# The second attention's projections: latent keys normed inside the query projection, tile by tile, with q's norm factor applied at the mask

## The reference

```python
kv_a = rms_norm(x, kv_norm) @ kv_w_a                      # 256 latent + 64 rotary columns
c_kv = rms_norm(kv_a[..., :256], kv_c_norm)
kv   = (c_kv @ kv_w_b)        # 8 heads x (128 key + 128 value)
k    = rms_norm(concat(kv keys, k_pe), kv_k_norm); rotary on its last 64 columns
q    = rms_norm((rms_norm(h @ w_q_a, q_a_norm) @ w_q_b), q_norm)   # 8 heads x 192, rotary on the last 64
p    = masked_softmax(q . k * 192 ** -0.5)
out  = (p @ v) @ w_out
```

## Time and profile before

| | us |
|---|---|
| median of three runs (lowest, highest) | 1888.21 (1884.53, 1888.35) |
| the profiled execution | 1888.43 |
| its span, first to last instruction | 1886.6 |
| TensorE busy in the span | 1729.1 (92%) |
| VectorE, ScalarE busy | 1229.9 (65%), 817.3 (43%) |
| mean granted clock of TensorE | 0.960 |

### The profile page before, as it was taken

The page is one execution under the profiler, slowest core; times in us unless marked ns, Lnnn a source line. Parts: engine busy times, 40 slices in busy tenths (PEclk is TensorE's granted clock), DMA queues, the critical chain, the costliest instruction groups (busy, mean ns, idle before and its releaser), DMA issues.

```text
span 1886.6 us, 29289 instructions
## 1 busy us (share of the span) xinstructions
PE 1729.1 (92%) x11365; PEld 1591.6 (84%) x11365; DVE 1229.9 (65%) x1751; ACT 817.3 (43%) x1199; POOL 39.3 (2%) x23
## 2 busy tenths in 40 slices
PE   7869999997697999999989869999899989689998
PEld 7857799996577999999988769999899989479997
DVE  4778566666767566666668956565766554866665
ACT  4556444335344333534353054334533344754433
POOL 0000000000005000000000000000000000000000
PEclk9979999998798999999999989999999999889999
DMA  7610345453223545455434034545354545035544
GB/s 265 212 45 1 99 171 198 174 193 102 99 68 133 192 175 200 146 190 198 177 142 161 1 122 168 195 172 200 146 189 178 196 138 178 2 101 202 199 171 162
DMA packets 53291, 285.93 MB, mean 152 GB/s; under 512 B 5872, under 2 KB 6128, under 8 KB 30704
## 3 DMA queue, kind: packets, MB, share of 16 engines
q1 hardware_dynamic: 52224, 281.46, 41.5%
q0 software_dynamic: 1008, 3.67, 0.5%
HBM read 284.05 MB, written 1.05 MB: 151 GB/s over the span
## 4 chain that ended last, share of the span: by engine, by line
PE 82%; DVE 11%; ACT 4%; issue 2%; DMA 0%; DVEq 0%; SPq 0%; ACTq 0%
PE bank L827 18%; PE bank L828 17%; PE bank L829 17%; PE bank L987 9%; PE bank L956 3%; PE bank L958 3%; PE bank L960 3%; DVE proj L1743 3%; PE bank L841 2%; PE bank L1044 1%; PE bank L1003 1%; ACT whi L437 1%; PE bank L1024 1%; DVE nmax L1477 1%; DVE att L1475 1%
## 5 line engine op out<-in xcount | busy, mean ns | idle before, releaser
L827 PE MATMUL bank<-hthi,whi 128*128 128x256 f32 x2144 | 607.9, 284 | 1.9 <-DVE wlo L1274 1.8
L828 PE MATMUL bank<-htlo,whi 128*128 128x256 f32 x2144 | 607.2, 283 | 0.0
L829 PE MATMUL bank<-hthi,wlo 128*128 128x256 f32 x2144 | 607.1, 283 | 0.0
L1268 DVE TENSOR_TENSOR wlo<-raw,whi 128x2048 fp32r<-128x2048 f32 x175 | 401.4, 2294 | 97.5 <-ACT whi L437 97.3
L827 PEld LDWEIGHTS bank<-hthi,whi 128*128 128x128 f32 x2144 | 411.7, 192 | 7.3 <-DVE wlo L1274 2.2
L828 PEld LDWEIGHTS bank<-htlo,whi 128*128 128x128 f32 x2144 | 411.6, 192 | 4.7
L829 PEld LDWEIGHTS bank<-hthi,wlo 128*128 128x128 f32 x2144 | 411.6, 192 | 0.0
L437 ACT ACTIVATE whi<-raw 128x2048 fp32r<-128x2048 f32 x175 | 333.9, 1908 | 34.8 <-PE bank L829 27.3
L509 ACT ACTIVATE tr<-tr 128x256 f32<-128x256 f32 x132 | 55.1, 418 | 657.8 <-DVE tr L1352 657.8
L1352 DVE TENSOR_TENSOR tr<-bank,rb 128x512 f32<-128x512 f32 x132 | 91.2, 691 | 231.8 <-PE bank L829 231.6
L1274 DVE TENSOR_TENSOR wlo<-raw,whi 128x1024 fp32r<-128x1024 f32 x174 | 214.5, 1233 | 25.5 <-ACT whi L445 25.1
(11 more groups left out here) (241 smaller groups left out, 2088.9 us busy)
## 6 DMA issues: line engine op xcount, KB each, us to landing
raw<-in_stream SPq DMA_DIRECT2D x176, 1024.0 KB, 5.3
raw<-in_stream SPq DMA_DIRECT2D x176, 512.0 KB, 3.5
wide<-in_wide POOLq DMA_DIRECT2D x7, 512.0 KB, 4.1
x<-in_x SPq DMA_DIRECT2D x1, 1024.0 KB, 5.4
out<-x SPq DMA_DIRECT2D x2, 512.0 KB, 2.9
wide<-in_const SPq DMA_DIRECT2D x1, 960.0 KB, 15.5
const<-in_const SPq DMA_DIRECT2D x1, 897.0 KB, 12.7
cols<-in_cols SPq DMA_DIRECT2D x1, 340.0 KB, 7.8
```

The lines of the kernel that those rows point to most:

```text
L827: nc.tensor.matmul(out, whi_, mhi, start=start, stop=False)
L828: nc.tensor.matmul(out, whi_, mlo, start=False, stop=False)
L829: return nc.tensor.matmul(out, wlo_, mhi, start=False, stop=stop)
L1268: V.tensor_tensor(wlo[:, s, 0:UA], raw[:, s, 0:UA], whi[:, s, 0:UA].bitcast(F32), ALU.subtract)\
```

## The change

- U_QA's piece b is split ahead of op_bq on ScalarE and VectorE; the eviction of U_KVA stands behind op_bq's first pair. The transposes of the latent keys (op_ckv) are issued by TensorE inside the step of U_QA, ahead of its chunk 6. Their high and low parts go to the buffers hidhi and hidlo (otherwise a feed-forward block's), not hthi and htlo, and come before the eviction of U_QA.
- The four KVB and QB units run as `step_by_tile`: all chunks of tile 0, then all of tile 1. The end of tile 0 raises a new semaphore s_half, upon which ScalarE evicts it (`evict_first`) while tile 1 runs. Tile 0 of the next unit waits for ScalarE's eviction only, tile 1 for VectorE's. U_KVB waits for both at its start. The transposes of op_qa come between U_KVB and U_KVB+1.
- k's sums and scaling come ahead of VectorE's eviction of U_QB+1. q's squares are taken by ScalarE per head and tile with an accumulator, 16 instructions of 192 columns in place of two of 1536, eight after U_QB and eight after the k copies; VectorE's sums go away.
- q isn't scaled by its norm factor. The factor times 192^-0.5 is the scalar of the mask instruction, which becomes one per tile. The rotary part of q is formed one tile at a time, and the low part of U_MO's piece a stands behind it, ahead of the q copies.

```diff
-            operand("op_bq", [(c, col("b_attn_norm", c)) for c in range(DC)], U_KVA + 1)
+            hi_b(U_KVA)
+            hi_a(U_QA)
+            norm(2)
+            hi_b(U_QA)
+            operand("op_bq", [(c, col("b_attn_norm", c)) for c in range(DC)], U_KVA + 1,
+                    after_first=lambda: evict(U_KVA, lambda t, u, c, w: kva[:, t, c:c + w], 2))
...
-            step(U_QA, lambda t, u, c, w: qa[:, t, c:c + w], 2)
+            hi_a(U_KVB)
+            hi_b(U_KVB)
+            operand("op_ckv", [(c, col("kv_c_norm", c)) for c in range(2)], 0, out=hidhi)
+            evict(U_QA, lambda t, u, c, w: qa[:, t, c:c + w], 2)
...
-            operand("op_ckv", [(c, col("kv_c_norm", c)) for c in range(2)], U_QA + 1)
+            hi_a(U_KVB + 1)
+
+            def evict_first(u, dst):
+
+                act.wait_ge(s_half, u - U_KVB + 1)
+                for j, (c, w) in enumerate(STEPS[u][2]):
+                    ins = nc.scalar.activation(dst(0, u, c, w), acc[plan[u][0][0][j]][:, 0:w], ACT.Copy)
+                ins.then_inc(s_eva, 1)
...
+            def q_squares(u):
+
+                act.wait_ge(s_eva, plan[u][2])
+                act.wait_ge(s_evd, plan[u][3])
+                for t in range(NT):
+                    for h in range(4 * (u - U_QB), 4 * (u - U_QB) + 4):
+                        at = 6144 + (4 * t + h % 4) * QK
+                        ins = nc.scalar.activation(tr[:, at:at + QK], q2[:, t, h, :], ACT.Square,
+                                                   accum_out=ss[:, 16 + 8 * t + h:17 + 8 * t + h])
+                return ins
+
+            evict_first(U_KVB, kv_out)
+            hi_b(U_KVB + 1)
             operand("op_qa", [(2 + c, col("q_a_norm", c)) for c in range(3)], U_QA + 1)
-            for u in (U_KVB, U_KVB + 1):
-                step(u, lambda t, u, c, w: kv[:, t, 4 * (u - U_KVB) + c // 256:4 * (u - U_KVB) + (c + w) // 256, :])
+            hi_a(U_QB)
+            evict_first(U_KVB + 1, kv_out)
+            hi_b(U_QB)
+            hi_a(U_QB + 1)
+            hi_b(U_QB + 1)
+            act.wait_ge(s_eva, plan[U_KVB + 1][2])
             act.wait_ge(s_evd, plan[U_KVB + 1][3])
-            act.wait_ge(s_eva, plan[U_KVB + 1][2])
             for t in range(NT):
                 ins = nc.scalar.activation(tr[:, 3072 + t * 1024:3072 + (t + 1) * 1024].rearrange("p (h n) -> p h n", h=H2),
                                            kv[:, t, :, 0:NOPE], ACT.Square)
             ins.then_inc(ev["k2_sq"], 1)
...
-            step(U_QB, q2_out)
+            evict_first(U_QB, q2_out)
+            own(q_squares(U_QB))
             act.wait_ge(ev["k2_ss"], 1)
             sqrt("k2n", 16, QK, EPS)
-            step(U_QB + 1, q2_out)
-            act.wait_ge(s_evd, plan[U_QB + 1][3])
-            act.wait_ge(s_eva, plan[U_QB + 1][2])
-            for t in range(NT):
-                nc.scalar.activation(tr[:, t * 1536:(t + 1) * 1536].rearrange("p (h n) -> p h n", h=H2),
-                                     q2[:, t, :, :], ACT.Square).then_inc(ev["q2_sq"], 1)
-            act.wait_ge(ev["q2_ss"], 1)
-            sqrt("q2n", 16, QK, EPS, 16)
+            hi_a(U_MO)
+            evict_first(U_QB + 1, q2_out)
...
+            own(q_squares(U_QB + 1))
+            sqrt("q2n", 16, QK, EPS, 16)
             attention("mla")
...
+            def step_by_tile(u, hi, lo, k0):
+
+                kk, pitch, pieces = STEPS[u]
+                s, end = u % 2, pieces[-1][0] + pieces[-1][1]
+                banks, before, _, _ = plan[u]
+                pe.wait_ge(s_loa, u + 1)
+                for t in range(NT):
+                    if t == 0 or u == U_KVB:
+                        pe.wait_ge(s_eva, plan[before][2])
+                    if t == 1 or u == U_KVB:
+                        pe.wait_ge(s_evd, plan[before][3])
+                    lhs = slice(t * P, (t + 1) * P)
+                    for k in range(kk):
+                        if t == 0 and k == kk - 1:
+                            pe.wait_ge(s_lob, u + 1)
+                        for j, (c, w) in enumerate(pieces):
+                            sl = slice(k * pitch + c, k * pitch + c + w)
+                            ins = mm3(acc[banks[t][j]][:, 0:w], hi[:, k0 + k, lhs], lo[:, k0 + k, lhs],
+                                      whi[:, s, sl], wlo[:, s, sl], k == 0, k == kk - 1)
+                        if t == 1 and k == kk - 2:
+                            ins.then_inc(s_usea, 1)
+                    ins.then_inc(s_useb if t else s_half, 1)
...
+            def qa_ready(k):
+
+                bq_ready(k)
+                if k == 6:
+                    pe.wait_ge(ev["ckv_ready"], 1)
+                    operand("op_ckv", lambda t, c: kva[:, t, c * P:(c + 1) * P], 2)
+
+            step(U_QA, ready=qa_ready)
+            taken("op_ckv", 1)
+            step_by_tile(U_KVB, hidhi, hidlo, 0)
             pe.wait_ge(ev["qa_ready"], 1)
             operand("op_qa", lambda t, c: qa[:, t, c * P:(c + 1) * P], 3)
+            step_by_tile(U_KVB + 1, hidhi, hidlo, 0)
             taken("op_qa", 2)
-            for u in (U_KVB, U_KVB + 1):
-                step(u)
             for u in (U_QB, U_QB + 1):
-                step(u, 2)
+                step_by_tile(u, hthi, htlo, 2)
...
-            pe.wait_ge(ev["q2n_ready"], 1)
+            pe.wait_ge(s_eva, plan[U_QB + 1][2])
+            pe.wait_ge(s_evd, plan[U_QB + 1][3])
...
+                dve.wait_ge(s_useb, u + 1)
+                if dst is not None:
+                    evict(u, dst, m)
+
+            def evict(u, dst, m=None):
+
                 banks = plan[u][0]
                 dve.wait_ge(s_useb, u + 1)
-                if dst is not None:
...
                     if kind == "mla":
-                        own(V.scalar_tensor_tensor(out=out, in0=src, scalar=float(QK) ** -0.5,
-                                                   in1=const[:, KO["mask"]:KO["mask"] + 512].rearrange("p (t n) -> p t n", t=2),
-                                                   op0=ALU.mult, op1=ALU.add))
+                        mask = const[:, KO["mask"]:KO["mask"] + 512].rearrange("p (t n) -> p t n", t=2)
+                        for b in range(2):
+                            at = 16 + 8 * b + i
+                            ins = V.scalar_tensor_tensor(out=out[:, b, :], in0=src[:, b, :], scalar=rs[:, at:at + 1],
+                                                         in1=mask[:, b, :], op0=ALU.mult, op1=ALU.add)
+                        own(ins)
...
+            lo_b(U_KVA)
+            lo_a(U_QA)
+            rstd("n2", 2, at=NORM)
+            lo_b(U_QA)
+            operand("op_bq", [(c, col("b_attn_norm", c)) for c in range(DC)],
+                    lambda: evict(U_KVA, lambda t, u, c, w: kva[:, t, c:c + w], 2))
...
-            step(U_QA, lambda t, u, c, w: qa[:, t, c:c + w], 2)
+            lo_a(U_KVB)
+            operand("op_ckv", [(c, col("kv_c_norm", c)) for c in range(2)], hi=hidhi, lo=hidlo)
+            lo_b(U_KVB)
+            evict(U_QA, lambda t, u, c, w: qa[:, t, c:c + w], 2)
...
-            operand("op_ckv", [(c, col("kv_c_norm", c)) for c in range(2)])
-            operand("op_qa", [(2 + c, col("q_a_norm", c)) for c in range(3)])
+            lo_a(U_KVB + 1)
...
-            for u in (U_KVB, U_KVB + 1):
-                step(u, lambda t, u, c, w: kv[:, t, 4 * (u - U_KVB) + c // 256:4 * (u - U_KVB) + (c + w) // 256, :])
-            step(U_QB, q2_out, between=k_sums)
-            rstd("k2n", 16)
-            step(U_QB + 1, q2_out)
-            k_scaled()
-            for t in range(NT):
-                dve.wait_ge(ev["q2_sq"], t + 1)
-                ins = V.tensor_reduce(ss[:, 16 + 8 * t:24 + 8 * t], tr[:, t * 1536:(t + 1) * 1536].rearrange("p (a n) -> p a n", n=QK),
-                                      AX, ALU.add)
-            ins.then_inc(ev["q2_ss"], 1)
-            rstd("q2n", 16, at=16)
-            for t in range(NT):
-                ins = V.tensor_tensor(q2[:, t, :, :], q2[:, t, :, :], per_head(16 + 8 * t, QK), ALU.mult)
-            ins.then_inc(ev["q2n_ready"], 1)
...
+            def rope(t):
+
                 for q in range(4):
-                    src = q2[:, t, :, NOPE + (q % 2) * hr:NOPE + (q % 2 + 1) * hr]
...
+                own(ins)
                 V.tensor_tensor(qpe[:, t, :, 0:hr], pr[t][0], pr[t][1], ALU.subtract)
-                ins = V.tensor_tensor(qpe[:, t, :, hr:ROPE], pr[t][2], pr[t][3], ALU.add)
-            ins.then_inc(ev["qpe_ready"], 1)
+                return V.tensor_tensor(qpe[:, t, :, hr:ROPE], pr[t][2], pr[t][3], ALU.add)
+
+            rope_rows()
+            evict(U_KVB, kv_out)
+            operand("op_qa", [(2 + c, col("q_a_norm", c)) for c in range(3)])
+            lo_b(U_KVB + 1)
+            lo_a(U_QB)
+            lo_b(U_QB)
+            evict(U_KVB + 1, kv_out)
+            lo_a(U_QB + 1)
+            lo_b(U_QB + 1)
+            evict(U_QB, q2_out)
+            k_sums()
+            rstd("k2n", 16)
+            k_scaled()
```

(28 more changed lines are left out.)

61 lines of the change are left out of this document (32 added, 29 removed).

## The result

The changed kernel took 1879.41 us in the median of four executions (1864.94 to 1894.02), the kernel before 1886.76 beside it (1884.53 to 1888.35). No execution lies near that median: two took 1864.9 and 1865.6, two 1893.2 and 1894.0. The ratio, 0.9887 with an interval of 0.9863 to 0.9911, is that of the short executions alone. The profiled execution is a short one: 1865.6 us, its span 1863.8.

A forecast was written before the change was run, and what follows sets the result against it. Hand-overs between engines were taken to bound the projections and norms, TensorE the attention. Scores 17.0 us earlier, less 0.2 (mask split) and 0.4 (clock), gave 1888.4 - 16.4 = 1872.0 us, range 1868 to 1878.5.

The forecast's parts named there:

- The front half: Projections up to the end of the first query projection: U_QB was to end at 478.7 us.
- The wait ahead of U_KVB: Before the first latent projection: TensorE newly waits 2.2 us for VectorE's queue, with U_KVB starting at 454.5.
- The wait in U_KVB+1: Inside the second latent projection: TensorE newly waits 3.3 us for VectorE's second weight piece.
- the 2.3 us of half clock behind it: Rest of U_KVB+1 after its wait: TensorE's matmuls at half clock, costing 2.3 us.
- half clock in U_KVB: First latent projection: none in the forecast; the dearer rival (0.21) had 2.3 us in its first tile, about half hidden.
- The back half: From the end of U_QB to the scores: VectorE's queue takes 20.6 us.
- The attention's tail: Last head's mask step, now two instructions: 0.2 us more, paid once.
- The sum: Whole kernel: scores start 17.0 us earlier, less 0.2 and 0.4, so 16.4 us gained.
- "Nothing" for loads, the stages behind and the second query projection's cover: Moved loads bind nothing, later stages don't lose the gain, and U_QB+1 ends about 3 us before VectorE evicts it.
- given back: Rival: stages behind are timed by loads or GpSimd's work, so the time stays 1888; chance 0.05.
- the term for the clock behind the wait ahead of the q copies: First scores after TensorE's longer wait: 0.4 us lost to the clock, between 0 and 2.5.
- the slower rival: Longer wait ahead of the q copies leaves attention at 1.2 GHz, up to 25 us more: 1897; chance 0.04.

The follow-up runs named there:

- e5: Changed kernel plus 30 split-precision matmuls nobody reads in TensorE's wait ahead of the last q transposes: 1868.09 us, ratio 0.9902.
- e4: Changed kernel with the mask step as one instruction over both tiles instead of two: median 1893.07 us, six of seven executions long.
- e1_again: The changed kernel run once more without an edit: median 1893.5 us of seven (1864.87 to 1894.78), the profiled execution 1893.63.
- e7: Kernel before with only the low part of U_MO moved to just ahead of the q copies: 1905.02 us, ratio 1.0109.
- e6: Changed kernel with U_MO's low part behind the q copies and 13 unread split-precision matmuls in the remaining wait: 1869.12 us, ratio 0.9915.
- e10: Kernel before with U_MO's low part moved ahead of the q copies, plus thirty unread split-precision matmuls in the wait: 1889.65 us, ratio 1.0017.
- e12: Changed kernel with 24 unread split-precision matmuls right behind the last q transposes, ahead of the first scores: 1876.91 us, ratio 0.9945.
- e8: Changed kernel with U_KVB to U_QB+1 running both tiles together per chunk again: median 1890.04 us, four executions at 1870.4 to 1877.2.
- e2_mo_late: Changed kernel with the low part of U_MO put behind the q copies: medians 1883.32 and 1883.94 us, ratios 0.9992 and 0.9983.
- e3: Changed kernel plus 30 unread plain fp32 transposes in TensorE's wait ahead of the last q transposes: 1872.32 us, ratio 0.994.

## Why the prediction was right and wrong

**The front half** held. U_QB's eviction came at 475.78, 477.5 on the scale of before, where I had 478.7. The wait ahead of U_KVB is 2.42 (2.2 predicted), ended by VectorE's eviction as said, with U_KVB at 455.4 on that scale (454.5). The wait in U_KVB+1 is 2.07, not 3.3, and the 2.3 us of half clock behind it did not come in this execution; they did, in part, in e5, where that piece's first matmul took 0.80 and U_QB's low part came 1.3 later. Against that stands half clock in U_KVB (0.63 for a matmul instead of 0.39), for which I had taken none: it ran for 7.2 us (453.64 to 460.82) instead of 5.6. The terms of the clock in the front were off by 1.6 and 2.3 us with opposite signs, and that they nearly cancel is luck.

**The back half** held nearly to the tenth. From U_QB's eviction to the scores it took 20.99 us, 20.6 predicted. Squares with their accumulator reads follow each other at 0.35 us, as estimated; k's root comes 0.4 us behind the sums (0.3). The second rotation, the low part of U_MO (2.2) and the copies stand in the predicted order without a gap.

**The attention's tail** costs 0.19 more (528.59 - 496.77 = 31.82 against 547.94 - 516.31 = 31.63), 0.2 predicted. The Trainium skill ("VectorE: DVE Perf Modes", section "The TRN2 errata") has 120 cycles of fixed latency with a PSUM source, by my estimate 0.13 us for the second instruction, and e4 shows just that, 0.88 against 0.75; the rest of the step from 0.68 before to 0.88 comes with the scalar operand in a column.

**The sum**, 16.4 us predicted, is 17.6 in the stage. "Nothing" for loads, the stages behind and the second query projection's cover was right: the stages behind the first output-projection eviction are the same within 0.1, but for the convolution's. The chances add up to 0.91 for faster and 0.05 for given back, not to the 0.92 and 0.04 of the last line.

**What failed is the term for the clock behind the wait ahead of the q copies**: 0.4 us for the first scores, between 0 and 2.5. In the short execution it is 0 for the scores, in the long one 21.7. With it failed the weight of the slower rival, and so the median. I priced that rival rightly (scores at 1.2 GHz throughout, up to 25 us and 1897; it is 23.5 us and 1893 to 1895) and saw its place, the wait of 4 us (3.94), but gave it 0.04, as I read one row as a rule: after 4.94 us of matmuls the clock had come back. Those were the projection's split-precision matmuls. What follows the q transposes is the attention's fp32 work, and e1_again shows 46 us of it with the clock at 0.50, e7 shows 27 us. That the wait is the cause e5, e6 and e10 show: with the wait filled the long executions are gone. That the kind of work behind it matters is borne out by one trace, e12's, where split-precision matmuls behind the same half-rate transposes had full clock back 2.0 us after they began. It is no rule for all fp32 work: fp32 transposes had it back in the short execution (495.6) and in the kernel before (515.0). The Trainium skill ("TensorE: Matmul & The Clock Gate", section "What's actually happening") says that throttled is the default and activity releases it; I had taken the scores for such activity, and these runs speak against that reading of it. The same section says that the point of the change varies from run to run; the traces agree, as the clock fell 3.9 us into the wait in one execution and 2.6 us into it in another (e1_again). The price here is 1.3% to 1.6%.

So the sign was right for the short executions and wrong for the more frequent ones. Where I wrote of the expected gain as one number, it should have been two cases: the transposes that run at half clock behind the wait either see it come back before they end (1.70 us for the last eight) or not (1.94). The traces show one thing that goes with it. Where the clock fell within 0.4 us of the start of these transposes, it came back in them (the short execution, the kernel before, the profiled executions of e4 and e8); where it fell 1.2 to 2.3 us before, it didn't (e1_again, e12, e7). These are seven traces and no experiment, and why the clock falls at one point or the other is open.

**What stays open:** what the typical execution of e2_mo_late does, whose extra 15 us are half clock by an estimate over the span, but lie in no trace; whether the kernel before never had a long execution (none above 1891.7 among more than fifty) because its wait, 2.83 us, ended as the clock fell, which only one trace shows; and why the clock came back after 27 us in e7 and only near the end in e1_again.

## What to carry to other kernels

Look at what TensorE does right behind a wait that lowers its clock, not only at how long the wait is: where long fp32 work follows, an idle time of 4 us cost more than 20 here. Moving 2.3 us of another engine's work to a "free" place is not free if it lengthens such a wait; a few matmuls that nobody reads, in banks that are free, held the clock here and cost nothing that these runs can tell, as TensorE would have waited. And take several executions before a median is believed: here it fell into a gap between two groups.

## What the hardware showed that was not expected

- The attention's fp32 work at half clock: 46 us (e1_again) and 27 us (e7) without the clock coming back, with TensorE busy for 45.17 of the 46; the first 18.4 us of each are gapless scores of 256 columns, at 1.19 us for two instead of 0.67. In e1_again the clock came back at 544.1, among transposes and fp32 value products, in e7 at 545.1, in scores 1 us behind such value products.
- One wait of 3.94 us, two outcomes: the clock fell 3.9 us into it in the short execution and 2.6 us into it in e1_again.
- In e12 the clock came back 2.0 us into twenty-four split-precision matmuls of 256 columns.
- With thirty fp32 transposes in the wait all six executions stayed below 1879 (e3), and in the profiled one the clock was 1.00 from 486 to 548 us. fp32 transposes also brought it back from half, at 495.6 in the short execution and at 515.0 in the kernel before; gapless fp32 scores did not in 18 us.
- A square of 192 columns with its accumulator read follows the next at 0.35 us on ScalarE (0.40 for 256 columns).
